# Block 2's attention: rotations split into two steps over two pairs of tiles, and a step's output finished ahead of its fillers

## The reference, cut to what matters

```
q  = (rms_norm(c_q, q_norm_w) @ w_uq).reshape(B, L, 4, 128 + 64)
q  = concat([q[..., :128], apply_rope(q[..., 128:], cos, sin)])      # 4 heads, 64 rotated columns each
kv = (rms_norm(c_kv, kv_norm_w) @ w_ukv).reshape(B, L, 4, 128 + 128)
k  = concat([k_nope, broadcast(apply_rope(k_r, cos, sin))])          # one rotated key part for all heads
s  = einsum('bqhd,bkhd->bhqk', qb, k) * 192 ** -0.5
o  = einsum('bhqk,bkhd->bqhd', softmax(s), v)

apply_rope(t): t1, t2 = halves of 32 columns; [t1*cos - t2*sin, t2*cos + t1*sin]
```

## Time and profile before

| | before |
|---|---|
| median of 3 runs | 3913.2 us (3906.98 to 3915.26) |
| the profiled execution | 3908.01 us, of which the profile's span is 3906.3 us |
| PE busy | 3694.0 us, 95% of the span |
| DVE, ACT, POOL busy | 43%, 32%, 28% |
| mean granted clock of TensorE | 0.98 of full speed |

### The profile page before, as it was taken

How to read it: one execution, slowest core, us unless ns; L and a number is a source line. 1 busy time by engine, 2 the same in 40 slices (tenths; PEclk the granted TensorE clock), 3 DMA queues, 4 the chain that set the end, 5 groups by cost and what they waited for, 6 DMA issues and landing times. The chain is left out here.

```text
span 3906.3 us, 50688 instructions
## 1 busy us (share of the span) xinstructions
PE 3694.0 (95%) x20618; PEld 3257.6 (83%) x20618; DVE 1695.6 (43%) x3158; ACT 1269.0 (32%) x2893; POOL 1083.5 (28%) x794
## 2 busy tenths in 40 slices
PE   6999998999999999999899999989999999998998
PEld 5887887878887788788788888778988998998898
DVE  5434554433335453355523334564344345334433
ACT  3112443033341221144403344222245422234541
POOL 2633222312112354322222121235310013531012
PEclk9999999999999999999999999999999999999999
DMA  3121111411104311211141101432110022210012
GB/s 115 38 73 65 36 33 52 151 33 44 44 30 161 111 50 65 71 33 33 44 151 44 35 34 38 160 109 70 44 36 16 24 89 76 68 46 23 13 43 98
DMA packets 84617, 243.88 MB, mean 62 GB/s; under 512 B 10656, under 2 KB 24224, under 8 KB 84384
## 3 DMA queue, kind: packets, MB, share of 16 engines
q1 hardware_dynamic: 84384, 240.64, 18.2%
HBM read 190.07 MB, written 50.53 MB: 62 GB/s over the span
## 5 line engine op out<-in xcount | busy, mean ns | idle before, releaser
L2691 POOL TENSOR_SCALAR Whi<-stage 128x1024 fp32r<-128x1024 f32 (+5 forms) x268 | 274.7, 1025 | 2069.2 <-DMA stage<-wstream 1280.0
L1388 PE MATMUL pj<-Hhi,Whi 128*128 128x512 f32 x1640 | 662.4, 404 | 10.8 <-DVE Hlo L2125 3.6
L1388 PE MATMUL pj<-Hhi,Wlo 128*128 128x512 f32 x1640 | 645.1, 393 | 0.0
L1388 PE MATMUL pj<-Hlo,Whi 128*128 128x512 f32 x1640 | 643.6, 392 | 0.0
L2693 POOL TENSOR_TENSOR Wlo<-stage,Whi 128x1024 fp32r<-128x1024 f32 (+5 forms) x268 | 622.0, 2321 | 22.4
L1388 PEld LDWEIGHTS pj<-Hhi,Whi 128*128 128x128 f32 x1640 | 311.9, 190 | 81.3 <-ACT PT L1828 6.6
L1388 PEld LDWEIGHTS pj<-Hhi,Wlo 128*128 128x128 f32 x1640 | 310.7, 189 | 67.4
L1388 PEld LDWEIGHTS pj<-Hlo,Whi 128*128 128x128 f32 x1640 | 311.8, 190 | 59.6
L1388 PE MATMUL pS<-Hhi,Whi 128*128 128x512 f32 x792 | 315.5, 398 | 17.4 <-DVE Hlo L2125 9.9
L1388 PE MATMUL pS<-Hlo,Whi 128*128 128x512 f32 x792 | 313.3, 396 | 0.0
L1388 PE MATMUL pS<-Hhi,Wlo 128*128 128x512 f32 x792 | 313.1, 395 | 0.0
(11 more groups left out here) (429 smaller groups left out, 7471.0 us busy)
## 6 DMA issues: line engine op xcount, KB each, us to landing
stage<-wstream SPq DMA_DIRECT2D x228, 512.0 KB, 4.3
merged<-Mb SPq DMA_DIRECT2D x32, 512.0 KB, 2.9
Mb<-merged SPq DMA_DIRECT2D x32, 512.0 KB, 4.1
gates<-tmp SPq DMA_DIRECT2D x48, 256.0 KB, 2.2
TH<-gates SPq DMA_DIRECT2D x24, 512.0 KB, 6.0
xres<-X SPq DMA_DIRECT2D x16, 520.0 KB, 2.9
xr<-xres SPq DMA_DIRECT2D x16, 520.0 KB, 4.1
X<-xT SPq DMA_DIRECT2D x16, 256.0 KB, 7.7
```

The source lines that it names most:

```text
L1388: x = pe.e.matmul(ps, w[a][:, v.koff + k * P:v.koff + k * P + P], moving(v.of, b, k, v.t0, v.n), start=k == 0 and i == 0, stop=k == v.K - ...
L2691: pool.e.tensor_scalar(upper, stage, 1.0, 0.0, ALU.mult, ALU.add).then_inc(*pool.tick("whi", c))
```

## The change

1. `m.rt` becomes two pairs of tiles. The second pair lies in the space of `P20`, the P tile of even steps; the softmax of step 0 therefore waits for the last `lo` of rotation chunk 1.
2. A rotation is two units now. `rope2` ends with the rotated `t1`; a new unit `rope2_out` holds the wait for it, ACT's four `hi` and DVE's four `lo`. The key's rotation (`kr`) stays in one unit.
3. The opening is reordered: rotation chunks 0 and 1 (one on each pair), the output of 0, rotation chunk 2, `qn` 0 to 2, the output of 1, `kn` 0 and 1, the output of 2, `kn` 2, values 0 to 2, first scores and first softmax, values 3 and 4. The weight stream's order follows.
4. In the fillers the output unit comes right behind its rotation (`and_then`), and all three chunks use pair 0, as before.
5. In a step that has fillers, `finish2` of the step before is put ahead of them; in other steps its place is unchanged.

The two `rope2_out` at the end of the diff are ACT's and DVE's.

```diff
-    m.rt = [at(f"rt{i}", o + 4160 + 1408 * i, [P, 348]) for i in range(2)]; o += 4160 + 2816
+    m.rt = [[at(f"rt{i}", o + 4160 + 1408 * i, [P, 348]) for i in range(2)]]; o += 4160 + 2816
     r2 = o
+    m.rt.append([at(f"rt{i + 2}", o + 1408 * i, [P, 348]) for i in range(2)])
     m.P2 = [at(f"P2{i}", o + 4160 * i, [P, L2]) for i in range(2)]; o += 8320
...
     def rotate(self, u):
-        u["sw_free"], u["t1_free"] = self.rope
-        self.rope = [("rotated2", u.id), ("lo", u.id)]
+        u["pair"] = u.pair or 0
+        u["sw_free"], u["t1_free"] = self.rope[u.pair]
+        self.rope[u.pair] = [("rotated2", u.id), ("lo", u.id)]
...
-        def rope_units(h, rel):
+        def rope_units(h, rel, pairs=(0, 0, 0)):
+
+            units = self.in2("rope2", ("uq", l, 4 + h // 2), of="QN", K=3, ready=self.qn_ready, name="q", box={}, sets=self.rotate,
+                             emptied="cosine2", scale=-SCALE2)
+            for u in units:
+                u["pair"] = pairs[u.i]
             def sets(u):
-                self.rotate(u)
-                qr[h] = qr[h + 1] = ("lo", u.id)
-            return self.in2("rope2", ("uq", l, 4 + h // 2), of="QN", K=3, ready=self.qn_ready, name="q", box={}, sets=sets,
-                            emptied="cosine2", scale=-SCALE2, rel=rel, dst=(0, 1) if h == 0 else (0, 2))
+                qr[h] = qr[h + 1] = ("lo", u.of.id)
+            return units, [Unit(kind="rope2_out", of=u, rel=rel, dst=(0, 1) if h == 0 else (0, 2), sets=sets) for u in units]
...
-        ro, v = rope_units(0, []), v_units(0)
-        self.run([ro[0], v[0], ro[1], v[1], ro[2], v[2]])
+        (ro, out), v = rope_units(0, [], (0, 1, 0)), v_units(0)
+        self.run(ro[0:2])
+        self.add(out[0])
+        self.add(ro[2])
         self.run(q_units(0, []))
-        self.run(v[3:] + kv_units(0, []))
+        self.add(out[1])
+        kv = kv_units(0, [])
+        self.run(kv[0:2])
+        self.add(out[2])
+        self.run(kv[2:] + v[0:3])
+        p_free[0] = ("lo", ro[1].id)
...
         scores(0)
         soft(0)
+        self.run(v[3:])
         gate(0, 0)
...
-                later = rope_units(2, [("scores2", scored[8].id)])
+                later, out = rope_units(2, [("scores2", scored[8].id)])
                 v = v_units(2)
                 self.fillers += v[:3] + [later[0], v[3], later[1], v[4], later[2]]
+                for x, y in zip(later, out):
+                    x["and_then"] = y
...
-                self.fill(99)
-            self.fill(2 if h == 1 and 2 < q < 6 else 1)
+
+            ahead = bool(s and self.fillers)
+            if ahead:
+                finish(s - 1)
+            self.fill(99 if q == 7 else 2 if h == 1 and 2 < q < 6 else 1)
             u = self.put("values2", **geometry(s), turns=turned[s].id, v_ready=vtok[h], po_free=self.po_free)
             valued[s] = u
             if s:
-                finish(s - 1)
+                if not ahead:
+                    finish(s - 1)
...
+    def rope2_out(u):
+        v, t1 = u.of, m.rt[u.of.pair][1]
+        t = slice(v.t0, v.t0 + v.n)
+        act.wait_ge(("rotated2", v.id))
         for x in u.rel:
             act.wait_ge(x)
+        phase_met(u)
         for h, r in enumerate(ROWS):
             for i in range(2):
-                hi(m.qr[u.dst[h]][0][ROWS[i], t], t1[r, 0:n], u.id, h, i)
+                hi(m.qr[u.dst[h]][0][ROWS[i], t], t1[r, 0:v.n], v.id, h, i)
...
+    def rope2_out(u):
+        v, t1 = u.of, m.rt[u.of.pair][1]
+        t = slice(v.t0, v.t0 + v.n)
+        dve.wait_ge(("rotated2", v.id))
         for x in u.rel:
             dve.wait_ge(x)
         for h, r in enumerate(ROWS):
-            dve.wait_ge(("hi", u.id, h, 1))
+            dve.wait_ge(("hi", v.id, h, 1))
             for i in range(2):
-                lo(m.qr[u.dst[h]][1][ROWS[i], t], t1[r, 0:n], m.qr[u.dst[h]][0][r, t], u.id, h, i)
-        dve.mark("lo", u.id)
+                lo(m.qr[u.dst[h]][1][ROWS[i], t], t1[r, 0:v.n], m.qr[u.dst[h]][0][r, t], v.id, h, i)
+        dve.mark("lo", v.id)
```

More of the change, by code:

```diff
@@ L1151, in latent @@
         self.run(gate(2))
-        self.rope = [None, None]
+        self.rope = [[None, None], [None, None]]
         u = self.in2("rope2", ("kr2", l), name="kr", box={}, sets=self.rotate, emptied="cosine2", scale=1.0, rel=[])
@@ L1902, in rope2 @@
         ps, n, t = m.pj[u.bank][:, 0:u.n], u.n, slice(u.t0, u.t0 + u.n)
-        sw, t1 = m.rt
+        sw, t1 = m.rt[u.pair]
         act.wait_ge(("proj", u.id))
@@ L1908, in rope2 @@
             act.e.activation(sw[i:i + 32, 0:n], ps[j:j + 32, :], ACT.Copy).then_inc(*act.tick("swapped", u.id, i))
-        act.wait_ge(("rotated2", u.id))
         if u.name == "kr":
+            act.wait_ge(("rotated2", u.id))
             hi(m.KR[ROWS[0], t], t1[ROWS[0], 0:n], u.id)
-            return
+    def rope2_out(u):
+        v, t1 = u.of, m.rt[u.of.pair][1]
+        t = slice(v.t0, v.t0 + v.n)
+        act.wait_ge(("rotated2", v.id))
         for x in u.rel:
             act.wait_ge(x)
+        phase_met(u)
         for h, r in enumerate(ROWS):
             for i in range(2):
-                hi(m.qr[u.dst[h]][0][ROWS[i], t], t1[r, 0:n], u.id, h, i)
+                hi(m.qr[u.dst[h]][0][ROWS[i], t], t1[r, 0:v.n], v.id, h, i)
     def pair(u):
@@ L2045, in scalar_program @@
              "pool1": pool_z, "unfold": unfold, "pool_out": pool_out, "values_in": values_in, "soft2": soft2,
-             "turns2": turns2, "values2_rest": values2_rest, "finish2": finish2}
+             "turns2": turns2, "values2_rest": values2_rest, "finish2": finish2, "rope2_out": rope2_out}
     for u in order.units:
@@ L2482, in rope2 @@
             *dve.tick("rotated2", u.id))
-        dve.wait_ge(("rotated2", u.id))
         if u.name == "kr":
+            dve.wait_ge(("rotated2", u.id))
             dve.wait_ge(("hi", u.id))
             lo(m.KR[ROWS[1], t], t1[ROWS[0], 0:n], m.KR[ROWS[0], t], u.id)
-            return
+    def rope2_out(u):
+        v, t1 = u.of, m.rt[u.of.pair][1]
+        t = slice(v.t0, v.t0 + v.n)
+        dve.wait_ge(("rotated2", v.id))
         for x in u.rel:
@@ L2671, in vector_program @@
              "pool0": pool0, "pool1": pool1, "unfold": unfold, "mark3": mark3, "pool_out": pool_out, "soft2": soft2,
-             "turned_last": turned_last, "values2_rest": values2_rest, "finish2": finish2, "last": last}
+             "turned_last": turned_last, "values2_rest": values2_rest, "finish2": finish2, "last": last,
+             "rope2_out": rope2_out}
     for u in order.units:
```

## The result

| | before | changed |
|---|---|---|
| median of 9 runs | 3907.3 us (3903.6 to 3920.6) | 3896.3 us (3888.6 to 3904.9) |
| ratio | | 0.9968, 95% interval 0.9956 to 0.9981 |
| the profiled span | 3906.3 us | 3886.9 us |
| first swap to first scores, layers 0 and 1 | 25.5 and 25.4 us | 18.5 and 18.2 us |
| first to last softmax minimum (36 steps), layers 0 and 1 | 238.9 and 240.5 us | 242.1 and 240.4 us |

The ratio is a gain of 12.5 us (7 to 17). The profiled span fell by 19.4 us, but 6.2 us of that is there before the first swap of layer 0 (2875.70 against 2881.86), 3.4 us lies between the two attentions and 1.2 us goes the other way behind the second; none of that work was touched. The two attentions themselves give 11.1 us: 14.1 in the openings, less 3.2 lost in the steps of layer 0, and 0.2 more gained in those of layer 1.

The account below looks back on a forecast made before the run. ACT's and DVE's round trip, not PE, bounds the attention's opening. Per layer -7.4 (opening) + 1.1 (clock) + 0.3 (steps) = -6.0 us, two layers -12.0: 3908.0 to 3896.0 profiled, about 3901 on the runs' scale; range 3893 to 3909.

Parts of the forecast that it names:

- What bounds the opening: First swap to first scores: ACT's and DVE's queues, 16.4 us each, not PE; 18.1 us against 25.5, -7.4 a layer.
- POOL beside DVE: Opening: POOL splits four weights while DVE is nearly always busy, stretching DVE's operations; +1.2 us taken, bounds 0 to 3.6 less 0.4.
- the 0.4 of the first sine: Opening, rotation of chunk 0: the sine beside a POOL pass at 0.82 instead of 0.44 us, already counted in DVE's queue.
- the 0.5 for handovers: Opening: 0.5 us added to the 16.4 because ACT's and DVE's queues feed each other.
- Banks: Opening: PE waits for banks, `kn` 2 for chunk 2's cosine, values 0 for the `lo` of `qn` 0; 1.7 and 0.7 us, under DVE.
- The clock in the opening: PE idle 3 to 4 us before the scores may drop to half clock; +1.1 us a layer, bounds 0 to +4.
- `kn` matmuls at full clock: Opening: a listed sign of the forecast, that the `kn` matmuls, at half clock before, would run at full clock.
- Values 3 and 4 in the softmax gap: Behind the first scores: their 2.1 us of PE fit in its 2.8 us wait for the first softmax and cost nothing.
- PE's 7.4 us on `yt`: Rotation steps: three PE waits that only lie beside the ACT and DVE chain; rival 2, counting them in full, about 3885, chance 0.06.
- 1.4 less 0.8: Rotation steps: -1.4 us for taking `yt` out of the chain, +0.8 for PE's transpose and projection ahead of the next rotation.
- The six plain filler steps: Steps with fillers but no rotation: PE waits 0.15 us before the transpose for P's copy; +0.9 us a layer.
- The forecast for the steps: All steps, from putting the output ahead of the fillers: +0.3 us a layer, bounds -0.5 to +4.

Follow-up runs that it names:

- POOL held: Changed kernel with `finish2` behind the fillers, POOL waiting for the first softmax's minimum before splitting head 1's two weights: ratio 0.9947 to the kernel before; opening 17.45 and 16.9 us.
- the output ahead alone: Changed kernel with the old opening (one pair, rotation and output together, values between), `finish2` still ahead of the fillers: ratio 1.0001 to the kernel before.

## Why the prediction came out as it did

The forecast was 12.0 us less, 3901 on the scale of the three runs shown, in a range of 3893 to 3909; measured were 3896.3 and, by the ratio, 12.5 us less. The nine runs of the kernel before have a median 5.9 us below that of the three, so on their scale the forecast is 3895.3. The sign, the place and the size were right; what held and what did not, by the stated steps:

1. *What bounds the opening.* Right. Sum 18.1 us, measured 18.5 and 18.2, with DVE's queue on the chain in layer 0 and both queues, ACT's for 9.6 us, in layer 1. That PE is not the limit is shown by five values units in front at 0 to 0.5 us.
2. *POOL beside DVE.* The mechanism is shown by POOL held, the size was low: +1.2 us was taken besides the 0.4 of the first sine, and the two last passes alone cost 0.9 and 1.4. In layer 0 the third operation of rotation 0 took 1.43 for 0.52 beside the long pass of the values' weight, too. All that DVE's operations took too long, the first sine apart, is 2.3 us in layer 0 and 2.2 in layer 1. The sum came out all the same because the 0.5 for handovers does not show and the other terms are a little high: 16.4 and 2.3 are already more than the 18.5 measured. That is luck, of about 1 us a layer.
3. *Banks.* `kn` 2 waited 2.7 us, not 1.7: the cosine of chunk 2 stands in DVE's queue behind the `lo` that POOL stretched. It lay under DVE's queue, as said. The wait of values 0, put at 0.7, was 0.2 in layer 1 and none in layer 0.
4. *The clock in the opening.* +1.1 us a layer was charged and nothing paid in the changed kernel: the half clock fell on `kn` 2 and the first values, where PE has slack, and the scores ran at full clock (layer 0, columns as in the earlier trace rows):

```profile
2888.00:2889.00 1.00, 1.00 (x7) 1.00 (x6) 0.97 (x3) 0.98 (x3) 0.92 (x2) 0.50 0.08 16
...
2895.00:2896.00 1.00, 1.00 (x8) 1.00 (x7) 0.00 (x0) 0.00 (x0) 0.00 (x0) 1.00 0.00 0
```

So the sign "`kn` matmuls at full clock" failed for `kn` 2. The 3 to 4 us of idle PE in front of the scores were 1.4 and 1.2, since 2.7 and 2.3 of idle lay in front of `kn` 2 and the half clock stretched what came between. Of the 18 layers of the nine profiles with the new order of the opening, the first scores ran at half clock in five and took 0.9 to 2.1 us more for it. The bounds were right, the value was luck either way.

5. *Values 3 and 4 in the softmax gap.* Right, 5.47 us against 5.48.
6. *PE's 7.4 us on `yt`.* Right that they are not the step's price: with the output ahead alone the time does not move, and the waits reappear in front of L1654 and L1640. The three rotation steps gained 1.04 and 1.18 us where 1.4 less 0.8, so 0.6, was forecast. The half clock did show between the first rotation and the second of layer 0 (1.85 us for nine matmuls, 1.44 at full clock); the step of 10.47 there is 0.2 us longer than that of layer 1.
7. *The six plain filler steps.* This is the term that was mis-sized: 0.15 was taken for each, from the waits on P's copy, and 0.44 was paid, 2.6 us a layer instead of 0.9. The wait itself was 0.24 us, and what was left out is that the transpose behind it takes 0.29 instead of 0.10. The forecast for the steps was +0.3 a layer, and by the table it is 2.6 - 1.1 = +1.5, with the clock behind rotation 2 adding 1.5 in layer 0 and giving 1.7 in layer 1.

Points 4 and 7 went opposite ways, a loss of 1.1 a layer charged and not met, and one of 1.2 met and not charged; that the total is within 0.5 us of the ratio's, and 0.9 of the trace's 11.1, is partly that. The interval of 7 to 17 us would not tell such a miss.

The half clock behind the rotation steps is the rule, and not as even a chance as the traces of before and changed make it look. Nine profiles of the study are of kernels with rotation and output in one step, 18 layers in all. The step behind rotation 2 ran at full clock in three of them (5.80 to 5.90 us) and in part at half clock in the other fifteen (7.2 to 8.7 us). The forecast had it in its upper bound only. With rotation and output in different steps the granted clock is 1.00 in every microsecond of the steps, in both layers of both such kernels. What decides on which side of a given wait it falls stays open.

## What to carry to other kernels

Where two engines hand one tile back and forth and both are half idle, list each one's operations and put independent work of both between the halves of a round; by the start of the scores the second buffer was worth 2 us a layer here, the order 5. A wait that the profile shows for one engine is worth what the chain through it says: moving what it waits for moved 7.4 us of waiting to other lines and gained 1. And where PE sets the step, put a unit with a fresh wait behind filler work, not in front: ahead of the fillers it cost 0.44 us each time; only in the rotation steps, which ACT and DVE set, did it gain. Spreading the two halves of a rotation over two steps gave back 8 to 10 us a layer, partly because PE stayed at full clock throughout.

## What was not expected of the hardware

- A `lo` or rotation operation of DVE with both inputs in SBUF takes up to 0.9 us more beside a splitting pass of POOL (a pair of `lo` 1.87 for 1.07, the third operation of a rotation 1.43 for 0.52), and the time of the `lo` returned when the pass was moved. Two `qnlo`, which read PSUM, kept their 0.93 beside such a pass (with the pass of 0.73 us from 2902.97).
- PE at half clock after a wait of about 3 us in one layer and at full clock after the same wait in the other: 1.6 us in one step, and 2.9 between the two layers of the output ahead alone (8.73 and 5.81). In the changed kernel, behind rotation 2 of layer 0 (busy us by 1 us of PE, PEld, DVE, ACT, POOL; then the granted clock):

```profile
3015.00:3016.00 1.00, 1.00 (x11) 1.00 (x10) 0.10 (x2) 1.00 (x4) 0.00 (x0) 0.96 0.00 0
3016.00:3017.00 1.00, 1.00 (x7) 1.00 (x6) 0.39 (x2) 0.83 (x3) 0.00 (x0) 0.50 0.00 0
```
